# Query rows of the samples copied to all partitions through a small DRAM buffer instead of by selector matmuls

## What is computed

```python
        k_past = cache_k[l][page_table].reshape(Bs, past_len, A_HEADS, A_HEAD_DIM)
...
        gate = jnp.einsum('bhtd,bhnd->bhtn', q_blk.astype(jnp.float32), k_mean)
...
        _, idx = lax.top_k(gate, top)
...
        s_sel = jnp.einsum('bhtd,bhtjsd->bhtjs', q_blk, k_sel, preferred_element_type=jnp.float32) * scale
```

## Time and profile before

| | |
|---|---|
| time before, median of 3 runs | 705.93 us (704.39 to 707.53) |
| time of the profiled execution | 707.18 us |
| its span, first to last instruction | 705.5 us |
| PE busy | 689.1 us (98%) |
| DVE busy | 445.2 us (63%) |
| POOL busy | 322.5 us (46%) |
| ACT busy | 296.2 us (42%) |
| mean granted TensorE clock | 0.993 of full |
| moved by transfers | 100.41 MB |
| K pages | 64 transfers of 256 KB from SP, median 3.6 us to landing |

### The profile page before, as it was taken

How to read it: one execution, slowest core, us unless ns; L and a number is a source line. 1 busy time by engine, 2 the same in 40 slices (tenths; PEclk the granted TensorE clock), 3 DMA queues, 4 the chain that set the end, 5 groups by cost and what they waited for, 6 DMA issues and landing times.

```text
span 705.5 us, 15197 instructions
## 1 busy us (share of the span) xinstructions
PE 689.1 (98%) x5563; PEld 643.3 (91%) x5563; DVE 445.2 (63%) x890; ACT 296.2 (42%) x568; POOL 322.5 (46%) x233
## 2 busy tenths in 40 slices
PE   6999999989999999999999999999999999999996
PEld 6999888869677777999999999999999999999996
DVE  4488889975342637527688684856748576575233
ACT  6542735445362223236555445334334434334222
POOL 6739999803232344345417708044170532606431
PEclk9999999989999999999999999999999999999999
DMA  7935997942764868743203323323233321413103
GB/s 244 298 121 165 290 291 240 275 117 64 238 211 138 256 207 277 123 150 112 69 2 116 108 77 121 120 69 112 62 125 110 111 81 66 158 65 120 60 1 122
DMA packets 88633, 100.41 MB, mean 142 GB/s; under 512 B 5374, under 2 KB 64338, under 8 KB 88570
## 3 DMA queue, kind: packets, MB, share of 16 engines
q1 hardware_dynamic: 74566, 92.91, 41.8%
q10 hardware_dynamic: 14004, 6.67, 3.8%
HBM read 92.92 MB, written 6.64 MB: 141 GB/s over the span
## 4 chain that ended last, share of the span: by engine, by line
PE 78%; DVE 10%; ACT 4%; POOL 3%; issue 3%; DMA 1%; ACTq 0%; SPq 0%; DVEq 0%; POOLq 0%
PE acc L915 7%; PE acc L916 6%; PE acc L917 6%; PE acc L1419 5%; PE acc L1418 5%; PE acc L1420 5%; PE scr L1419 3%; PE scr L1420 3%; PE scr L1418 3%; PE scr L1385 3%; PE scr L1384 3%; PE scr L1386 3%; PE acc L1384 3%; PE acc L1385 3%; PE acc L1386 3%
## 5 line engine op out<-in xcount | busy, mean ns | idle before, releaser
L915 PE MATMUL acc<-act_hi,w_hi 128*128 128x256 f32 (+1 forms) x416 | 122.9, 296 | 0.0
L2020 POOL TENSOR_TENSOR h_lo<-relu,h_hi 128x520 fp32r<-128x520 f32 x32 | 44.2, 1384 | 165.0 <-ACT h_hi L1805 164.7
L916 PE MATMUL acc<-act_lo,w_hi 128*128 128x256 f32 (+1 forms) x416 | 118.5, 285 | 0.0
L917 PE MATMUL acc<-act_hi,w_lo 128*128 128x256 f32 (+1 forms) x416 | 118.3, 284 | 0.0
L1504 POOL TENSOR_TENSOR w_lo<-raw,w_hi 128x1024 fp32r<-128x1024 f32 x24 | 57.3, 2389 | 101.5 <-ACT w_hi L1497 99.0
L1973 POOL TENSOR_TENSOR prod<-kv,Qb 128x1024 f32<-128x1024 f32 x32 | 85.5, 2707 | 17.6 <-DVE S L2206 11.5
L915 PEld LDWEIGHTS acc<-act_hi,w_hi 128*128 128x128 f32 x416 | 79.5, 191 | 5.6 <-issue 5.1
L916 PEld LDWEIGHTS acc<-act_lo,w_hi 128*128 128x128 f32 x416 | 79.6, 191 | 0.0
L917 PEld LDWEIGHTS acc<-act_hi,w_lo 128*128 128x128 f32 x416 | 79.4, 191 | 0.0
L2523 DVE TENSOR_TENSOR xT<-acc,xT 128x260 f32<-128x260 f32 x64 | 26.6, 424 | 48.4 <-PE acc L1420 48.4
L2504 DVE TENSOR_TENSOR zT<-acc,rstd 128x264 f32<-128x264 f32 (+1 forms) x56 | 23.5, 422 | 52.8 <-PE acc L917 50.2
(11 more groups left out here) (422 smaller groups left out, 2301.8 us busy)
## 6 DMA issues: line engine op xcount, KB each, us to landing
kv<-in_cache_k_dram SPq DMA_DIRECT2D x64, 256.0 KB, 3.6
kv<-in_cache_v_dram SPq DMA_DIRECT2D x64, 256.0 KB, 3.0
raw<-in_w_up_dram SPq DMA_DIRECT2D x16, 1024.0 KB, 5.4
raw_d<-in_w_down_dram SPq DMA_DIRECT2D x12, 1024.0 KB, 5.1
raw<-in_w_in_dram SPq DMA_DIRECT2D x14, 512.0 KB, 6.0
raw<-in_w_in_dram SPq DMA_DIRECT2D x7, 1024.0 KB, 6.8
x_tok<-in_x_prompt_dram SPq DMA_DIRECT2D x8, 512.0 KB, 5.5
raw<-in_w_out_dram SPq DMA_DIRECT2D x4, 1024.0 KB, 6.9
```

Of the source, the lines that this page charges most:

```text
L915: pe.matmul(out, W_HI[home(g)][:, k, :], hi[k][:, cols], start=(n == 0), stop=False)
L916: pe.matmul(out, W_HI[home(g)][:, k, :], lo[k][:, cols], start=False, stop=False)
L917: mm = pe.matmul(out, W_LO[home(g)][:, k, :], hi[k][:, cols], start=False, stop=(n == KT - 1))
L2020: pool.tensor_tensor(h_lo[:, t, :], relu2[:, t % 2, :], h_hi[:, t, :].bitcast(F32), ALU.subtract).then_inc(s_hs_lo, 1)
```

## The change

The selector matmuls, their copies from PSUM and the split of the rows are gone. ACT copies the bank of `qs_tok` to `q_rows` (8 rows of 2 KB), and starts a transfer of it to a DRAM buffer `q_dram` (16 KB). SP then starts, for each sample, one transfer that reads the sample's row from `q_dram` 128 times, once for each partition of `Qb[:, b % 2, :]` (256 KB written). POOL waits for that transfer where it waited for the ACT copy. In `LOADS` the rows of samples 0 and 1 have the key 5.6, and the row of sample b >= 2 has `chunk_slot(4 * b - 5) + 0.59` and waits until all chunks of sample b - 2 have been multiplied. The order of SP's list around the new entries, with chunk numbers at K:

```diff
-    at(5, ("qb", 0), ("qb", 1), ("rows_f",), ("rows_sum",))
+    at(5, ("rows_f",), ("rows_sum",))
...
-        if n % 4 == 1 and n >= 5:
-            at(chunk_slot(n), ("qb", n // 4 + 1)) if n // 4 + 1 < NS else None
...
+    x += [(5.6, ("q", b)) for b in range(2)] + [(chunk_slot(4 * b - 5) + 0.59, ("q", b)) for b in range(2, NS)]
...
-        qs_split, _ = place("qs_split", [LOW + NS, AW], F32R, at=z_slot(20))
+        q_rows, _ = place("q_rows", [NS, AW], at=z_slot(20))
+        q_dram = nc.dram_tensor("q_dram", (NS, AW), F32, kind="Internal").ap()
...
+                elif what == "q":
+                    b, = a
+                    sp.wait_ge(s_q_out, 16)
+                    if b >= 2:
+                        sp.wait_ge(s_kmul_ok, 4 * (b - 1))
+                    sp.dma_start(Qb[:, b % 2, :], q_dram[b:b + 1, :].broadcast_to([P, AW])).then_inc(q_in[b % 2], 16)
...
-                elif name == "qb":
-                    b, = a
-                    evacuated(pe, "qs_tok", 0)
-                    pe.wait_ge(s_sel_ok, 3)
-                    out = open_job(pe, "qb", b, 0)
-                    done(pe.matmul(out, every(both[:, b:b + 1], LOW + NS), qs_split[:, :], start=True, stop=True))
...
                 elif name == "qs_tok":
-                    act.wait_ge(s_sel_ok, 3)
-                    act.activation(qs_split[0:NS, :], full(act, "qs_tok", 0)[0:NS, :], ACT.Copy)\
-                       .then_inc(s_qs_hi, 1)
+                    copy_out(q_rows[:, :], full(act, "qs_tok", 0)[0:NS, :], "qs_tok", 0)
+                    evacuated(act, "qs_tok", 0)
+                    act.dma_start(q_dram[:, :], q_rows[:, :]).then_inc(s_q_out, 16)
...
-                elif name == "qb":
-                    b, = a
-                    out = full(act, "qb", b, 0)
-                    if b >= 2:
-                        act.wait_ge(s_kmul_ok, 4 * (b - 1))
-                    copy_out(Qb[:, b % 2, :], out, "qb", b, 0)
...
                     if c == 0:
-                        evacuated(pool, "qb", b, 0)
+                        pool.wait_ge(q_in[b % 2], 16 * (b // 2 + 1))
```

More of the change, by code:

```diff
@@ L235, in plan @@
     scratch = {
-        "par2": 1, "rstd": 1, "xn": 1, "gates": 1, "gcols": 1, "qs_tok": 1, "qb": 1, "vs_tok": 1, "tokk": 1, "tokv": 1, "tokm": 2,
+        "par2": 1, "rstd": 1, "xn": 1, "gates": 1, "gcols": 1, "qs_tok": 1, "vs_tok": 1, "tokk": 1, "tokv": 1, "tokm": 2,
         "sm_prep": 2, "sm_c": 1, "sm_r": 1, "sm_rt": 1, "ml_m": 1, "ml_k": 3, "ml_o": 2, "ml_t": 1, "ml_mc": 1,
@@ L630, in build @@
         s_rrec = sem("rrec")
-        s_qs_hi = sem("qs_hi")
+        s_q_rows = sem("q_rows_ok")
+        s_q_out = sem("q_out")
+        q_in = [sem(f"q_in{i}") for i in range(2)]
         s_vs_hi = sem("vs_hi")
@@ L1594, in task @@
                 elif name == "qs_tok":
+                    copy_out(q_rows[:, :], full(act, "qs_tok", 0)[0:NS, :], "qs_tok", 0)
+                    evacuated(act, "qs_tok", 0)
+                    act.dma_start(q_dram[:, :], q_rows[:, :]).then_inc(s_q_out, 16)
+                elif name == "vs_tok":
                     act.wait_ge(s_sel_ok, 3)
-                    act.activation(qs_split[0:NS, :], full(act, "qs_tok", 0)[0:NS, :], ACT.Copy)\
-                       .then_inc(s_qs_hi, 1)
-                elif name == "vs_tok":
-                    act.wait_ge(s_sel_ok, 4)
                     act.activation(vs_split[0:NS, :], full(act, "vs_tok", 0)[0:NS, :], ACT.Copy)\
@@ L1943, in _ @@
                                pattern=[[1, 1]], channel_multiplier=-1).then_inc(s_ident_ok, 1)
-            for rows_split in (qs_split, M_split):
-                pool.memset(rows_split[:, :].bitcast(F32), 0.0).then_inc(s_sel_ok, 1)
+            pool.memset(M_split[:, :].bitcast(F32), 0.0).then_inc(s_sel_ok, 1)
             weight_lo(pool, 0, 0)
@@ L2176, in task @@
                     M = rows[:, 2, 0:SEQ]
-                    dve.wait_ge(s_sel_ok, 3)
+                    dve.wait_ge(s_sel_ok, 2)
                     dve.tensor_copy(M_split[0:MH, :], M).then_inc(s_M_split, 1)
@@ L2191, in task @@
                        .then_inc(s_srow_ok, 1)
-                elif name in ("qs_tok", "vs_tok"):
-                    rows_hi, made = (qs_split, s_qs_hi) if name == "qs_tok" else (vs_split, s_vs_hi)
+                elif name == "vs_tok":
                     out = full(dve, name, 0)
-                    dve.wait_ge(made, 1)
-                    free(dve.tensor_tensor(rows_hi[LOW:LOW + NS, :], out[0:NS, :], rows_hi[0:NS, :].bitcast(F32),
+                    dve.wait_ge(s_vs_hi, 1)
+                    free(dve.tensor_tensor(vs_split[LOW:LOW + NS, :], out[0:NS, :], vs_split[0:NS, :].bitcast(F32),
                                            ALU.subtract), name, 0)
@@ L2562, in slot_free @@
                 elif g == 20:
-                    full(dve, "qb", NS - 1, 0)
+                    dve.wait_ge(s_q_out, 16)
                 elif g == 21:
```

## The result

The kernel after takes 712.16 us (median of 5, 711.5 to 714.65) against 705.96 us of the kernel before on the same chip: ratio 1.0101, interval 1.0083 to 1.0119. The medians differ by 6.2 us, where +3.3 was forecast. Either way the kernel after is slower by more than the 0.5% (3.5 us) that the prediction took as the bound. The profiled execution took 714.65 us, with a span of 712.6 and 2.05 outside it; the one of before had 1.7 outside. 0.3 us of the difference thus lies outside the span, and no view explains it.

A forecast was written before the change was run, and what follows sets the result against it. The prediction took a POOL/DVE loop in the score stage, not PE, to bound the kernel. Terms of +1.6 by chunk 24 and +1.7 after gave +3.3 us on 705.93, so 709.2; range 704.3 to 713.

The forecast's parts named there:

- What bounds the kernel: Score stage: a POOL/DVE loop sets `page_max`; PE runs beside it, its lead worth at most 1.0 us.
- the rival that PE pays: Whole kernel: PE sets the end and all 3.9 us of removed matmuls come back, 702.0 us; chance 0.10.
- The start: Gate rows and chunk 0: chunk 0 at 40.9, scan blocked beside POOL, so the loop starts 1.2 us later.
- K10 and K12: SP's queue: q3 ahead of K10 waits for chunk 7, shifting later loads 2.7; less 1.3 slack, +1.4 at chunk 12.
- K18 and K19: Pages already late before; q4 and q5 put 0.5 MB before and among them, +1.0 us.
- The waits of POOL for DVE: POOL's waits for DVE after K18 and K19 take up 2.0 us of the delay by chunk 24.
- K26 to K29: SP's queue: q7 ahead of K26 waits for chunk 23, delaying pages up to K29; +1.7 us at chunk 29.
- the queue falls behind: Loads K12 to K31: DMA engines at 97% pass each delay on, 7 to 8 us, 713 us; chance 0.14.
- The slow clock: PE's 1.2 GHz stretch around 149 falls into waiting time, saving 2.4 us: 706.8 us; chance 0.08.

The follow-up runs named there:

- ScalarE's queue: Kernel after, with the transfers of samples 2 to 7 issued from ScalarE's queue instead of SyncE's: 709.57 us, ratio 1.0060; with 64 of 512 columns each, 706.74 us, 1.0017.
- the waits alone: Kernel after, with SyncE only waiting at the places of samples 2 to 7 and starting no transfer: 708.4 us, ratio 1.0055.
- 64 columns at the tied places: Kernel after, with 64 of 512 columns per transfer for samples 2 to 7, same queue places and waits: 712.98 us, ratio 1.0109; again 711.59 us, 1.0084.
- the kernel with the early rows: Kernel after, with each row in its own buffer, five transfers issued in the idle stretch and three ahead of the loaded one: 705.49 us, ratio 1.0002.

## Why the prediction was right and wrong

**What bounds the kernel: right.** The time followed `page_max`, and that followed POOL's chunks. The test without six selector matmuls gave 1.1 us at `page_max` where 1.0 was the bound, and the rival that PE pays (702.0) is out. That the two numbers agree so closely is luck in part, since 0.7 of it came by way of a K page.

**The start: right.** Chunk 0 at 41.08 against 40.9. Its two terms were each off: the write and its wait took 1.45 (36.1 to 37.55) where 2.0 was taken, the broadcast 3.46 where 2.8 was. The scan was blocked, 3.29 against 1.21, as I had taken, and the loop started 1.18 later (+1.2). Of this 0.25 is that the whole execution began later, so the chain's part is 0.9, and the close match with 1.2 is luck in part. It isn't left at the end: the kernel without the six transfers has the same start and a ratio of 0.9993.

**K10 and K12: the step that failed.** The mechanism was right, q3 ahead of K10, waiting for chunk 7, and so was its shift: K10 was issued 1.18 behind chunk 7 (forecast 1.15), and K12's first page 2.7 later than the start alone explains (forecast 2.7). The sum stopped there, and its term of +1.4 for chunk 12 is the one that failed. It took K12's second page to follow at the old distance, and it didn't: the first was held 2.65 us behind the unit instead of 1.17. Chunk 12 started 5.03 later, 3.85 without the start; +1.4 had been forecast. That term was mis-sized by 2.5 us, of which 1.5 is the longer hold and 0.3 the longer landing (4.32 against 4.01). The rest is chunk 12's slack: of the 1.3 us that I credited, about 0.6 was the time from the landing to the start (84.95 to 85.52 after), so only 0.7 were to be had. Chunk 12 has these 0.57 us in every run in which it waits for its page, where most other chunks start 0.12 after theirs; why is open. The hold of 1.17 was visible in the trace of before, as a page of 1.17 us where its neighbours have 0.33, and I read past it.

**K18 and K19: mis-sized.** +2.4 between chunk 12 and chunk 18 against +1.0, with another hold of 2.61 (1.39 before) and chunks 14 and 15 waiting for pages. The waits of POOL for DVE took back 1.3 by chunk 24 (2.0 forecast). At chunk 24 that makes +6.1 against +1.6: of the 4.5 us that the sum lacked there, 2.5 are chunk 12's, 1.4 those of chunk 18, and 0.7 what the waits for DVE didn't take back.

**K26 to K29: right in the step, luck in the sum.** Chunk 29 waited 1.64 us for its page (+1.7 forecast). From chunk 24 to the end it is +1.66, but that also holds a wait of 0.86 for a page at chunk 25, which the forecast didn't have, and shorter chunks, which took as much away.

**The rivals.** The one nearest in number, that the queue falls behind (713), named the engines at 97% busy as the cause. The runs show two causes, and neither is that alone. The two strict waits cost 0.0062 (4.4 us) alone, and 0.0043 (3.0 us) less when taken out of the kernel after. The bytes in the loaded stretch cost 0.0043 (3.0 us) on ScalarE's queue and 0.0048 (3.4 us) on SyncE's, where the number of rows went from 128 to 1 with them. Six queue entries cost about 1 us. Going step by step from the kernel after to the one without transfers, 3.0 + 3.4 + 1.2 = 7.6 us is the whole gap; this sum closes because the steps follow each other, and proves nothing more. With 4.4 for the waits it would be 9.0, which would mean that the costs overlap: a page that is late for one reason isn't late again for the other. Each of these differences is uncertain by 0.2 to 0.3% of the time, so neither the overlap nor which cause is larger is shown. In the single traces the waits alone moved `page_max` by 1.2 us and their removal by 2.8, the bytes by 1.5 on ScalarE's queue (116.0 against 114.5) and by 4.9 on SyncE's (118.4 against 113.5). What isn't settled is why 64 columns at the tied places (1.0084 and 1.0109) gain so little over full rows.

**The slow clock: no gain, and its part is open.** A rival had PE's stretch at the lower of its two clock levels (1.2 GHz) fall into waiting time. It didn't: it lies right behind `page_max` in both profiled executions, and is as long in both. A mean granted clock of 0.66 over 10 us is 6.8 us at the lower level; before, 0.73 and 0.93 make 6.8 too. New is a stretch of 3.4 us in 50 to 60 (0.83, before 1.00). The first two lines are of the kernel before, the others of the kernel after.

```profile
145.00:155.00 10.00, 8.19 (x41) 6.89 (x40) 6.45 (x19) 3.87 (x9) 1.50 (x4) 0.73 0.23 58
155.00:165.00 10.00, 10.00 (x69) 8.90 (x68) 4.81 (x11) 6.44 (x13) 3.10 (x5) 0.93 0.63 179
...
50.00:60.00 10.00, 8.80 (x64) 8.58 (x63) 8.05 (x17) 2.00 (x4) 5.98 (x3) 0.83 0.54 151
...
155.00:165.00 10.00, 7.92 (x34) 7.07 (x35) 5.62 (x17) 2.65 (x7) 0.25 (x1) 0.66 0.48 130
```

The spans tell what it costs: from `page_max` to the end it took 553.5 to 553.9 us in the four kernels whose clock didn't fall there, 555.0 to 555.1 in the five with 3.4 us at the lower level, and 556.2 to 556.9 in the five with 6.8 us, before and after among them. That is 3 us for such a stretch, where the rival had 2.4. The length of the wait doesn't decide alone whether the clock falls: PE waits 1.20 us for the gate rows in the kernel after and in all its variants (0.78 before), and the clock fell behind that wait in six of these eleven traces; behind a wait of 0.98 for `page_max` it fell in the kernel before, behind one of 0.99 in the kernel with six matmuls less it didn't. Averaged over a run the clock was at or above 0.998 in 43 of 92 runs of the kernel before (median 704.6 us) and in none of the five of the kernel after. At a mean clock of 0.995 to 0.997 the medians are 706.2 (41 runs) and 711.6 (2 runs), 5.4 us apart. By these two runs some 1 us of the 6.2 would be that the kernel after meets lower clocks more often; that isn't shown, and the forecast had nothing for it.

## What to carry to other kernels

A transfer put into an in-order queue brings its wait along, and that wait holds everything behind it: put it behind every entry that needs less, since two waits that were one chunk too strict cost here 0.4 to 0.6% of the time, about as much as 1.6 MB of traffic in a loaded stretch. Small data that is known early should be loaded while the DMA engines are idle, into whatever is free at that time; the same six transfers cost 7 us inside the loaded stretch and nothing measurable ahead of it. When a shift is carried down a queue, look at each entry's own length there: one of 1.17 us among entries of 0.33 is already being held, and need not keep its length when more stands ahead of it.

## What the runs showed of the hardware

- A scan with both operands in SBUF is blocked beside POOL's two-operand multiplication like an ordinary tensor operation: 3.29 us against 1.21. So is one of 4x8 elements: 2.31 against 0.14. Moving POOL's work moves the block to whatever instruction is next; it doesn't remove it. The Trainium skill, SBUF — State Buffer, section "SBUF: two separate sides", has the pair of ports as an exclusive lock, and these rows agree.
- On SyncE the next page goes out 1.1 to 1.3 us after a query row's transfer, with 128 rows (70.22 to 71.33 in the kernel after) or with one (58.49 to 59.75), and 1.1 after another page. The row itself takes less: five rows in turn went out within 2.24 us (38.24 to 40.48 in the kernel with the early rows), and a page, a row and a page at 58.22, 58.81 and 59.90, where two pages are 1.10 apart. So a row adds 0.4 to 0.6 us.
- In the loaded stretch the first page behind a weight unit is held at its issue for 0.5 to 2.7 us. The hold ahead of chunk 12 was 2.65 and 2.70 with a full row in the queue just before, 1.55 to 2.34 with 64 columns, 0.50 and 0.60 with one row, 0.56 to 1.46 with none, and 1.69 with full rows on ScalarE's queue. Elsewhere it varied between like kernels (2.19 ahead of chunk 18 without any transfer), so what fills the queue isn't only this.
- A row of 2 KB brought to 128 partitions (256 KB written) took 3.1 to 3.5 us to land as the first transfer on idle engines; K pages of 256 KB, from 128 different rows, took 2.7 to 2.9 at 42 to 46 us in the kernel before.
- Outside the span lie 1.7 us in the kernel before and its variants and 2.1 in the kernel after and its variants, but again 1.7 in the two that start the six transfers from ScalarE's queue. Its cause is open.
